# Weaving the first light expert's up slots between the slots of the first expert pass

## The reference, cut to what matters

```python
def moe_swiglu(h, router_w, w1, w3, w2):
    logits = (xf @ router_w).astype(jnp.float32)
    top_val, top_idx = lax.top_k(logits, TOP_K)
    gates = jax.nn.softmax(top_val, axis=-1)
    ...
    def expert_block(args):
        tok_b, e = args
        return swiglu(x_pad[tok_b], w1[e], w3[e], w2[e])   # (silu(x w1) * (x w3)) w2
    ...
    y = y.reshape(P, D) * buf_g[:, None]
    out = jax.ops.segment_sum(y, buf_tok, num_segments=N + 1)[:N]
```

## Time and profile before

| | |
|---|---|
| time, median of 3 runs | 1384.54 us (1384.03 to 1385.4) |
| time of the profiled execution | 1380.48 us |
| its span, first to last instruction | 1378.6 us |
| mean granted TensorE clock | 0.987 |
| TensorE busy | 1316.9 us (96%) |
| VectorE busy | 913.9 us (66%) |
| ScalarE busy | 737.8 us (54%) |
| read from HBM | 472.46 MB, 343 GB/s over the span |

### The profile page before, as it was taken

How to read it: one execution, slowest core, us unless ns; L and a number is a source line. 1 busy time by engine, 2 the same in 40 slices (tenths; PEclk the granted TensorE clock), 3 DMA queues, 4 the chain that set the end, 5 groups by cost and what they waited for, 6 DMA issues and landing times.

```text
span 1378.6 us, 20762 instructions
## 1 busy us (share of the span) xinstructions
PE 1316.9 (96%) x8030; PEld 959.8 (70%) x8030; DVE 913.9 (66%) x1526; ACT 737.8 (54%) x1273; POOL 10.6 (1%) x45
## 2 busy tenths in 40 slices
PE   7999999999999999989999999998999999789987
PEld 5875899999888988728837888836845673157521
DVE  3688898888886759719839998907936760067401
ACT  4655654444474568519729998807925760057300
POOL 0000000000000020000000000000000000000000
PEclk9999999999999999999999999999999999999998
DMA  9985758889757258899999999999999969999997
GB/s 326 361 325 210 272 216 304 317 293 335 280 183 260 92 197 321 299 421 405 421 415 415 410 410 413 422 383 416 410 419 410 421 261 387 422 406 420 385 419 295
DMA packets 130145, 474.91 MB, mean 344 GB/s; under 512 B 9437, under 2 KB 11626, under 8 KB 107514
## 3 DMA queue, kind: packets, MB, share of 16 engines
q1 hardware_dynamic: 128672, 472.28, 87.6%
q10 hardware_dynamic: 1370, 1.25, 0.3%
HBM read 472.46 MB, written 1.05 MB: 343 GB/s over the span
## 4 chain that ended last, share of the span: by engine, by line
PE 80%; DMA 9%; DVE 6%; ACT 2%; SPq 2%; issue 1%; ACTq 0%; DVEq 0%
PE bank L1766 11%; PE bank L1769 11%; PE bank L1767 10%; PE bank L1867 5%; DMA beside_lo<-in_moe_w 3%; PE bank L1303 3%; PE bank L1300 3%; PE bank L1299 3%; DMA ring<-in_moe_w 2%; PE bank L1591 2%; PE bank L1861 2%; PE bank L997 2%; DMA beside_h<-in_moe_w 2%; PE bank L1678 2%; SPq L839 2%; PE bank L1343 2%
## 5 line engine op out<-in xcount | busy, mean ns | idle before, releaser
L3184 DVE TENSOR_TENSOR lo_first<-ring,hi_first 128x512 fp32r<-128x512 f32 x156 | 101.5, 684 | 18.9 <-ACT hi_first L2349 18.7
L3184 DVE TENSOR_TENSOR lo_second<-ring,hi_second 128x512 fp32r<-128x512 f32 x158 | 102.4, 684 | 10.0 <-ACT hi_second L2349 9.5
L2349 ACT ACTIVATE hi_second<-ring 128x512 fp32r<-128x512 f32 x158 | 97.6, 631 | 21.4 <-PE bank L1769 15.3
L2604 DVE SCALAR_TENSOR_TENSOR ada_acc<-ring,c_act,ada_acc 128x512 f32<-128x512 f32 x140 | 105.0, 750 | 3.9
L3184 DVE TENSOR_TENSOR lo_third<-ring,hi_third 128x512 fp32r<-128x512 f32 x158 | 102.6, 684 | 7.4 <-ACT hi_third L2349 6.7
L2349 ACT ACTIVATE hi_third<-ring 128x512 fp32r<-128x512 f32 x158 | 97.4, 631 | 10.1 <-PE bank L1769 3.5
L2349 ACT ACTIVATE hi_first<-ring 128x512 fp32r<-128x512 f32 x156 | 96.0, 631 | 8.5 <-PE bank L1769 3.1
L1867 PE MATMUL bank<-ring,work 128*32 128x512 f32 x642 | 86.8, 601 | 11.1 <-DMA ring<-in_moe_w 11.1
L1980 ACT ACTIVATE w_hi<-ring 128x1024 fp32r<-128x1024 f32 x66 | 68.8, 1053 | 46.1 <-PE bank L1348 23.4
L3360 DVE TENSOR_TENSOR work<-work,bank 128x512 f32<-128x512 f32 (+1 forms) x8 | 5.5, 686 | 130.5 <-PE bank L1867 130.5
L2839 DVE TENSOR_TENSOR w_lo<-ring,w_hi 128x1024 fp32r<-128x1024 f32 x66 | 79.3, 1220 | 9.8 <-ACT w_hi L1980 9.7
(11 more groups left out here) (564 smaller groups left out, 3294.1 us busy)
## 6 DMA issues: line engine op xcount, KB each, us to landing
ring<-in_moe_w SPq DMA_DIRECT2D x202, 1024.0 KB, 19.1
ring<-in_ada_w SPq DMA_DIRECT2D x24, 2048.0 KB, 12.3
ring<-in_moe_w SPq DMA_DIRECT2D x47, 768.0 KB, 12.1
ring<-in_ffn_w SPq DMA_DIRECT2D x15, 2048.0 KB, 8.9
beside_w<-in_moe_w SPq DMA_DIRECT2D x18, 1024.0 KB, 21.3
beside_x<-in_moe_w SPq DMA_DIRECT2D x17, 1024.0 KB, 18.8
beside_out<-in_moe_w SPq DMA_DIRECT2D x17, 1024.0 KB, 19.7
beside_lo<-in_moe_w SPq DMA_DIRECT2D x17, 1024.0 KB, 19.0
```

Source lines behind the costliest of these rows:

```text
L2349: A(hi_piece(Q), raw_piece(SPLITS[r], q, j), ACT.Copy).then_inc(hi_done, 1)
L2604: step = v.scalar_tensor_tensor(acc, w[:, k, :], c_act[:, k:k + 1], acc, ALU.mult, ALU.add)
L3184: v.tensor_tensor(lo_piece(Q), raw_piece(SPLITS[r], q, j), hi_piece(Q).bitcast(F32), ALU.subtract).then_inc(lo_done, 1)
```

## The change

The 16 up slots of light pass 1 no longer stand in one block behind slot 8 of pass 0. They are put in twos and threes between the slots 4 to 12 of pass 0 (`WOVEN`). The order of issue is now apart from the order of use: the first 17 halves issued are still slots 0 to 8 (first half) of pass 0, whose addresses are known, and from there on the order is that of use. A half's home is the one of the half that is used 17 places before it, so homes are no longer periodic. For the light up slots to come so early, their gather is at q = 9 instead of 35, the places of the tokens at 4 instead of 14, the dispatch at 6 instead of 20, the output gains at 5 instead of 12. The gates of the passes are split off and stand at 14. Light chunk 0 has banks 2 and 3 and a tile of its own for its raw values (`woven_raw`); its silu, product, turn and copy hang at q = 24 to 28 of pass 0. Those of chunk 1 hang behind the last up slot and at q = 48 to 52. `overflow_table()` is moved from in front of the light products to the start of the light down slots, behind the four additions of pass 0's output.

```diff
+WOVEN = ((0, 0, 4), (1, 0, 2), (0, 4, 5), (1, 2, 5), (0, 5, 6), (1, 5, 8), (0, 6, 9), (1, 8, 10), (0, 9, 10), (1, 10, 12),
+         (0, 10, 11), (1, 12, 14), (0, 11, 12), (1, 14, 16), (0, 12, 21), (1, 16, 23))
+WOVEN_SILU = {24: 0}
+WOVEN_PROD = {25: 0, 48: 1}
+WOVEN_TURN = {26: 0, 50: 1}
+WOVEN_TAKE = {27: 0, 51: 1}
+WOVEN_LOW = {28: 0, 52: 1}
...
-    run = []
-    for m in range(NE):
+    run = list(WOVEN)
+    for m in range(2, NE):
...
-    GAIN_AT = 12
-    TOKENS_AT = 14
-    MID_DISPATCH_AT = 20
+    GAIN_AT = 5
+    TOKENS_AT = 4
+    MEMBERS_AT = 14
+    MID_DISPATCH_AT = {0: 6, 3: 20, 5: 20}
...
-    MID_GATHER_AT = g_last["w3", 1] + 3
+    MID_GATHER_AT = {0: 9, 3: g_last["w3", 1] + 3, 5: g_last["w3", 1] + 3}
...
+    ahead = [(0, n // 2, n % 2) for n in range(len(HOMES))]
+    issued = ahead + [key for key in consumed if key not in ahead]
+    issue_no = {key: n for n, key in enumerate(issued)}
+    home_at, use_no = list(range(len(HOMES))), [0] * len(HOMES)
+    for n in range(len(HOMES), len(issued)):
+        left = issue_no[consumed[n - len(HOMES)]]
+        home_at.append(home_at[left])
+        use_no.append(use_no[left] + 1)
...
+            for n, (m, i, h) in enumerate(issued[:2 * len(STREAM)]):
+                if n >= len(HOMES):
+                    wait_left(sp, n)
...
+                load_expert_half(sp, ids[m], KINDS[m], i, h, n)
+                if n == len(HOMES) - 1 or (m, h) == (0, 1) and i >= PER - NE + 2:
                     j = len(ids)
                     sp.wait_ge(s_places, 1)
...
+                if m == 1 and end < LPER:
+                    if end == UPS:
+                        light_silu(m, 1)
+                    return
...
+                if m == 1:
+                    if first == UPS:
+                        overflow_table()
+                    return
```

More of the change, by code:

```diff
@@ L147, in build @@
     STREAM = [(m, i) for m, first, end in RUN for i in range(first, end)]
-    stream_no = {key: n for n, key in enumerate(STREAM)}
+    consumed = [(m, i, h) for m, i in STREAM for h in range(2)]
+    consumed += [(m, i, h) for m in range(NE, NE + OVER) for i in range(PER) for h in range(2)]
     finished = [m for m, first, end in RUN if end == ends[KINDS[m]]]
@@ L518, in build @@
         hidb = work[:, 1, 0:1024].rearrange("p (b n) -> p b n", b=2)
+        woven_raw = work[:, 1, 512:1024]
         xraw = work[:, 1, 0:512]
@@ L804, in own_width, with up_bank, light_raw @@
             return ECW[c] // 2
+        def up_bank(m, what, c):
+            if m == 1 and c == 0:
+                return 2 if what == "w1" else 3
+            return 0 if what == "w1" else 6
+        def light_raw(m, c):
+            return woven_raw if m == 1 and c == 0 else silu_e[:, 0, :]
         def columns_up(c):
@@ L905, in _ @@
             ids = [0]
[L906 to L916, removed]
+            for n, (m, i, h) in enumerate(issued[:2 * len(STREAM)]):
+                if n >= len(HOMES):
+                    wait_left(sp, n)
+                elif HOMES[n] >= HALVES:
+                    wait_vacated(BESIDE[HOMES[n] - HALVES])
+                elif HOMES[n] % 2 == 0:
+                    wait_used(order[PRE - SLOTS + HOMES[n] // 2])
+                load_expert_half(sp, ids[m], KINDS[m], i, h, n)
+                if n == len(HOMES) - 1 or (m, h) == (0, 1) and i >= PER - NE + 2:
                     j = len(ids)
@@ L1823, in light_turned @@
                 for j in range(FPC):
-                    last = nc.tensor.transpose(psum[4][:, j * P:j * P + rows], silu_e[0:rows, 0, turned_columns(j)],
+                    last = nc.tensor.transpose(psum[4][:, j * P:j * P + rows], light_raw(m, turn)[0:rows, turned_columns(j)],
                                                ident[0:rows, 0:rows])
@@ L1873, in light @@
                         spread(hosted, "B", (spreads[i],))
-                    if i in LIGHT_TURN and not first:
+                    if i in LIGHT_TURN and not first and m != 1:
                         light_turned(m, LIGHT_TURN[i])
-                    if i == end - 1 == UPS - 1:
+                    if i == end - 1 == UPS - 1 and m != 1:
                         light_turned(m, LCH - 1)
@@ L3338, in expert, with light_prod, light_low @@
                         gathered(group_in[m])
-                    if q == MID_LOW_AT + 1 and m in mid_group_in:
+                    if m in mid_group_in and q == MID_GATHER_AT[m] + 1:
                         gathered(mid_group_in[m])
             more = []
+            def light_prod(m, c):
+                rows = XT * columns_up(c)
+                own = light_raw(m, c)[0:rows, :]
+                dve.wait_ge(s_esl, chunk_no(m, c) + 1)
+                dve.wait_ge(slot_left, slots_done(m, last_slot["B"]["w3", c]))
+                v.tensor_tensor(own, own, psum[up_bank(m, "w3", c)][0:rows, :], ALU.mult).then_inc(s_ea, 1)
+            def light_low(m, c):
+                dve.wait_ge(s_hdh, chunk_no(m, c) + 1)
+                dve.sem_inc(s_hdl, 1)
             def light(m, hosted, first, end):
```

96 lines of the change are left out of this document (58 added, 38 removed).

## The result

The changed kernel takes 1373.5 us (median of 9 runs, 1371.17 to 1376.11), the kernel before 1382.5 us (9 runs, 1376.86 to 1385.4). The ratio is 0.9942, 95% interval 0.9929 to 0.9954: 0.6% faster, some 8 us by the ratio and 9.0 by the medians. The forecast was 5.4 us less at 1379.1, with a range from 1375.0. The sign was right and the gain was some 3 us larger than the sum (2.6 by the ratio, 3.6 by the medians). The time lies 5.6 us under the forecast and 1.5 us under the range. Of the 5.6 us, 2.0 come from the value that the gain was taken from: 1384.54 us was the median of three runs of the kernel before, and nine runs give 1382.5.

A forecast was written before the change was run, and what follows sets the result against it. TensorE was taken to bound 520 to 717 us, except at the light block's end, where it waits. 7.8 - 1.2 - 0.7 - 0.5 = 5.4 us less, 1384.54 to 1379.1 us; forecast's own range 1376.5 to 1381.5, overall 1375.0 to 1386.5.

The forecast's parts named there:

- (e): Lower clock behind the gather: its 1.8 us loss moves with the gather; if it stays away, 1.8 us more gained.
- (b): SiLU of light chunk 1 comes after slot 12's first splits, so TensorE waits: 0.7 us added, bounds 0 and 2.
- (a): TensorE changes between the two kinds of matmul 12 times more, at 0.1 us each: 1.2 us added.
- Removed, 7.8 us: TensorE's waits at the light block's end: 5.6 us for transfers, 1.1 for the product, 1.1 for ScalarE.
- The transfers' ledger: Landings of woven halves: narrowest behind slot 5 at 574.1 us, margin 1.4; last at 621.6, margin about 5.
- the rival by the transfers' rate: The mixture's transfers reach only 349 GB/s, so woven halves land late: slower, 1387.8 us, chance 0.05.
- the rival at 0.55: Changes of matmul kind: from 0.55 us each the gain is gone; at 1.10 us each 1391.1 us, chance 0.10.
- (c): `overflow_table()`, 4.65 us and hidden before, now follows pass 0's last addition and delays pass 2's start: 0.5 us added.
- (d): VectorE gets some 1.5 us of places and dispatch work in pieces 4 to 6: nothing net, bounds 1 us either way.
- (f): Gains, gather, places, turns and SiLU are the same instructions elsewhere: no cost.
- all of it reaches the end: From pass 2's start on, transfers wait for TensorE at the dips, so the whole 5.4 us gain lasts.
- "more" case: Changes, SiLU and table cost nothing, no clock loss behind the moved gather: 9.6 us less, 1374.9 us, chance 0.10.

The follow-up runs named there:

- block kernel: The kernel before, unchanged, with the light up slots in one block behind slot 8: 1382.5 us.
- the first repeat: The changed kernel profiled again with nothing changed: 1376.59 us, pass 0's first matmul to pass 2's first 192.74 us, one lower-clock stretch at 628 us.
- merged groups: The changed kernel with two pairs of light groups merged and the overflow table ahead of the last additions: 1373.03 us, ratio 0.994.
- early gather: The changed kernel's early places, dispatch, gains and gather, but the 16 light up slots in one block as in the kernel before: 1381.02 us, ratio 0.9995.
- woven variants: The changed kernel with early SiLU, early table, both, five light slots earlier, or merged groups: 1372.77, 1371.24, 1373.24, 1381.09, 1373.03 us.
- both fillers: The kernel before with unread matmuls in the light block's waits, four filler operations or one at a time: 1397.19 and 1381.48 us.
- both small edits: The changed kernel with SiLU of light chunk 1 at piece 45 and the overflow table ahead of the last additions: 1373.24 us, ratio 0.9942.
- light filler: The kernel before with one unread filler operation (two matmul records) in each wait of the light block's last halves: 1381.48 us, ratio 0.9998.
- early SiLU: The changed kernel with SiLU of light chunk 1 at piece 45 of pass 0, ahead of slot 12's splits: 1372.77 us, ratio 0.9943.
- early table: The changed kernel with the overflow table ahead of the four additions of pass 0's output: 1371.24 us, ratio 0.9925.
- the third repeat: The changed kernel profiled again with nothing changed: 1375.73 us, pass 0's first matmul to pass 2's first 194.10 us, lower-clock stretches at 541 and 630 us.

## Why the prediction was off

Two steps failed, and neither is a term of the weave itself. The base: "The median of the runs lies 4.06 us above the profiled execution, with no stage of its own that I can point to", and the gain was taken from that median of three. Over all 75 runs of this kernel the median is 1382.5 and the standard deviation of one run 2.4 us, so the three were a high draw, and 2.0 of the 5.6 us are this. The other is the clock, under (e).

The five profiles of each kernel give a ledger. The mean span went from 1380.8 to 1371.9 us, 8.9 us less.

*What the sum was about.* The block kernel's region is 197.28 us with one stretch (mean of three profiles) and 198.82 with two (mean of two): 1.54 us a stretch and 195.7 without. The changed kernel's is 189.97 without (mean of two). The repeats agree: 189.88 + 1.27 of longer wait + 1.54 = 192.7, measured 192.74; for the third 189.88 + 1.04 + 2 x 1.54 = 194.0, measured 194.10. With the mean wait of five (0.4 us more than in the first and fourth) the work of the region is 195.7 - 190.4 = 5.3 us shorter. The sum had 5.4, or 5.9 without the table's 0.5, which falls just behind the region's end. From the measured terms it would be 7.8 less 1.7 for (b) and 0.7 to 1.9 for (a), 4.2 to 5.4.

*Removed, 7.8 us.* Right in kind: no light half waits, and the product's and the turn's waits are gone. Its size was not measured by itself; it follows as 5.3 + 1.7 + (0.7 to 1.9) = 7.7 to 8.9.

*The transfers' ledger.* Right for the first profile. The narrowest half was forecast for 574.1 and landed at 572.8, the last woven one at 621.6 and landed at 620.5. The forecast margin of 1.4 us was 1.6 us there (the half's first matmul starts at 574.40). In the four repeats it was 0.04, 1.3, 0.75 and 1.1: in the first repeat the half landed at 574.50 and was used at 574.54. So that TensorE never waited there is partly luck. The rate was 419 to 421 GB/s from 560 us on, so the rival by the transfers' rate is out. The sign "540 to 560 us over 400 GB/s" was wrong (369), and 520 to 540 us fell from 280 to 246.

*(a) Changes of kind, 1.2 us.* By the starts of TensorE's matmuls a light group costs 0.09 us going in, 0.12 behind its last four matmuls and 0.11 at the next slot's first: 0.32 a group, 0.16 a change, 1.9 us for twelve. The merged groups gave 0.06 a change, 0.7 us. The forecast's 0.1 lies between them; the rival at 0.55 is out.

*(b) SiLU, 0.7 us with bounds 0 and 2.* Too small, and its upper bound too. It is 1.18, 2.45, 1.22, 2.22 and 1.39 us over the 0.52 in the five profiles, 1.7 in the mean. The mechanism was the one forecast; that it hangs on one landing, which moves by over a microsecond, was not.

*(c) The table, 0.5 us.* Measured 0.45 (0.46 by the run with the table early).

*(d), (f).* Nothing seen in the early gather's run, 1381.02 against 1382.57 with an interval over one.

*(e) The clock: the other step that failed.* "The gather only moves, so I let the loss move with it; if it stays away, 1.8 us more are gained." The first half holds: a stretch stands with the gather near 577 us in three of five profiles before and near 540 us in two of five after (and in all five woven variants, but not in the early gather's profile). What the step left out is that one execution shows one draw. The other repeats of the block kernel have a second stretch, behind the waits of the light block, which the weave takes away. In the region the count went from 7 in five profiles to 4, which at 1.54 us is 0.9 us.

The larger part lies where the prediction put nothing: behind pass 2's start no term stood for the clock. From pass 2's first matmul to the end the five profiles of before take 663.3 us in the mean, with 33.0 us at the lower clock; those of after 660.3 with 23.5. That is 3.0 us.

That these 3.0 us are the stretches, the traces show, since both kernels run the same instructions there. The time between two fixed instructions of ScalarE, in all 18 profiles (the instructions are named by their starts in the first profile of before):

| from, to, us | no stretch between | one of 3.4 us | one of 6.8 us |
|---|---|---|---|
| 894.64, 925.43 | 29.26 to 29.29 (12 profiles) | 30.79 to 30.88 (5) | 32.49 (1) |
| 1100.77, 1125.11 | 22.79 (5) | 24.32 to 24.42 (12) | 26.01 (1) |
| 1270.16, 1300.14 | 29.98 to 29.99 (9) | 31.56 to 31.58 (4) | 33.12 to 33.18 (5) |

The kernel makes no difference, only the stretch does, at 1.5 to 1.6 us for 3.4 us. Between the means of before and after, the stretches near 899, 940, 1114 and 1281 us make 1.25, 0.56, 0.63 and 0.95 us, 3.4 in all; the table takes 0.45 back, and all the rest adds 0.05. So the step "all of it reaches the end" holds: in the first profile the lead is 7.25 us from 767 to 894 us, through a stage where transfers run at 414 GB/s.

Why there are fewer stretches in the changed kernel is not settled, and that the weave removes them behind pass 2 is not shown. Four of the five of before have a stretch at 899 us, none of after has one there. But two woven variants have one at 892, and three block kernels, the early gather and both fillers, have none. The mean clocks say the same: 0.9861 for before (66 runs) and 0.9893 for the changed kernel (13), but 0.9863 and 0.9868 for two woven variants (both small edits, merged groups; 6 runs each) and 0.9884 for the light filler, whose slots are in one block (12). No run changed only the clock, and five draws a side may mislead.

So 5.3 - 0.3 (pass 0 starts at 519.64 us in the mean before and at 519.96 after) + 0.9 + 3.0 = 8.9 us; with the table on the side of the work it is 4.6 us of work and 4.3 of clock. A second way uses all times of these runs: fitted together, each kernel with its own level, the time falls by 0.73 us (standard error 0.08) for 0.001 of mean clock. At equal clock the changed kernel (13 runs) is 6.0 us faster (error 0.6) than the kernel before (66 runs); its mean clock is 0.0032 higher, 2.3 us. The two ways differ by 1.4 us for the work, some two errors of the fit. By the same fit the early SiLU, the early table, both together and the merged groups lie 1.4, 1.7, 2.3 and 2.1 us under the changed kernel, each with an error of 1 us, where 0.8 to 1.2, 0.4 to 0.5, 1.3 to 1.7 and 0.9 were expected. That the weave saves 4.6 to 6.0 us is firm, that the whole is 8 to 9 us owes 2.3 to 4.3 to a clock that nobody forecast.

The signs in the profile: right were the woven halves of 0.86 us without a wait, slot 12 near 628 (625.2 to 629.1), the table's small wait and the dip at 900 us that comes earlier. Pass 2's start was forecast near 712 and lies at 709.1 to 714.6, 711.6 in the mean. A sign of being wrong was to be "more than one stretch at the lower clock before 630 us"; the third repeat has two between 520 and 630 us and is still 7 us faster than before's mean. Wrong was the chain: it still has a load of 22 us, slot 12's, behind which the SiLU stands. And the lower end of the range, 1375.0, was the "more" case with (a) to (c) at nothing, taken from 1384.54; from 1382.5 it would be some 1373, and the time measured would lie just inside. The clock behind pass 2 was in no case.

## What to carry to other kernels

Work that waits for transfers is woven into work that is slower than its transfers, as long as each piece lands in time: a ledger of landings from issue times and one rate told here to 1.3 us where the margin was, and five light slots moved forward by one slot cost all that the weave brought. A term or a margin that hangs on a single landing gets the spread of that landing (over a microsecond here) and not one value. Where TensorE's clock varies from run to run, its share is read from several profiles of the kernel before, and a forecast of a few microseconds is taken from the median of more than three runs. Once both kernels run the same instructions again, the time between the same two instructions tells at once what a difference is made of.

## What the hardware showed unexpectedly

The granted clock falls to 0.50 for 3.4 or 6.8 us, six to ten times in an execution and once more in its last microseconds, at places that repeat from run to run (577, 617, 899 and 940 us before); of these only the one at 940 us is in all five profiles. A stretch of 3.4 us costs 1.54 us in the region and 1.5 to 1.6 us at three places behind it, less than half its length. Over all runs of the ten kernels the mean clock went from 0.979 to 0.992, worth nearly 10 us: more than the weave. Ahead of slot 12, a stretch followed where TensorE had waited for 2.04, 2.15 and 2.38 us in that same execution, and none where it had waited for 1.11, 1.15 and 1.31; three and three profiles, and no run set the wait by itself.
